# Silu of c in four pieces inside the projection, two opening blocks worked by input tile, longer warming runs: a transformer kernel on one core

## The reference, cut to what matters

```
h = rmsnorm(x, norm1_g)
proj = h @ w_in                     # dq, dk, dv, fq, fk, fv, fg
...                                 # two attentions, w_out, gated MLP
c_act = silu(c)                     # 1024 values
for l in 0, 1:
    sh_m, sc_m, g_m, sh_f, sc_f, g_f = split(c_act @ ada_w[l] + ada_b[l])
    h = modulate(rmsnorm(x, norm_g[l, 0]), sh_m, sc_m)
    y = conv mixer (l = 0) or latent attention (l = 1)
    x = x + g_m * rmsnorm(y, norm_g[l, 1])
    h = modulate(rmsnorm(x, norm_g[l, 2]), sh_f, sc_f)
    y = relu(h @ mlp_up_w[l]) ** 2 @ mlp_down_w[l]
    x = x + g_f * rmsnorm(y, norm_g[l, 3])
```

## Time and profile before

| | |
|---|---|
| median of 3 runs | 1792.23 us |
| profiled execution, its time | 1791.45 us |
| profiled execution, its span | 1789.7 us |
| time outside the span | 1.75 us |
| mean granted TensorE clock | 0.993 |
| weight blocks, KB each | 284, 512 |

### The profile page before, as it was taken

One profiled execution on the slowest core, in us unless ns is written; L12 is line 12 of the kernel. 1 busy time (PEld: TensorE's weight loads), 2 busy tenths in 40 slices (PEclk: granted clock), 3 DMA queues, 4 the chain that ended last, 5 costly groups with the idle time before them and its releaser, 6 DMA issues. The chain is left out here.

```text
span 1789.7 us, 22632 instructions
## 1 busy us (share of the span) xinstructions
PE 1746.8 (98%) x8124; PEld 1413.5 (79%) x8124; DVE 1094.8 (61%) x1603; ACT 632.2 (35%) x987; POOL 95.0 (5%) x155
## 2 busy tenths in 40 slices
PE   8989999999999999999999999999999999999996
PEld 7857677888888888887888888877767788888886
DVE  6676554655555576878656565667775865434354
ACT  4226444322222353244423142425444442323231
POOL 0000000000000000100100000010000100000001
PEclk9999999999999999999999999999999999999998
DMA  6421111444444434652245555521321234333221
GB/s 230 116 85 36 48 48 56 155 148 164 146 153 153 141 106 130 219 192 83 83 176 188 203 180 203 174 85 53 118 71 38 81 97 163 105 94 95 94 82 47
DMA packets 61951, 216.63 MB, mean 121 GB/s; under 512 B 7216, under 2 KB 9392, under 8 KB 61680
## 3 DMA queue, kind: packets, MB, share of 16 engines
q1 hardware_dynamic: 45072, 154.95, 25.7%
q0 software_dynamic: 16656, 60.04, 10.9%
q10 hardware_dynamic: 144, 0.59, 0.1%
HBM read 212.67 MB, written 2.10 MB: 120 GB/s over the span
## 5 line engine op out<-in xcount | busy, mean ns | idle before, releaser
L794 ACT ACTIVATE w_hi<-w_raw 128x1024 fp32r<-128x1024 f32 x284 | 299.0, 1054 | 409.0 <-PE psum L1952 372.1
L1950 PE MATMUL psum<-h_hi,w_hi 128*128 128x512 f32 x1080 | 421.4, 390 | 2.9 <-DVE h_lo L1200 2.9
L1952 PE MATMUL psum<-h_hi,w_lo 128*128 128x512 f32 x1080 | 420.2, 389 | 0.0
L1951 PE MATMUL psum<-h_lo,w_hi 128*128 128x512 f32 x1080 | 420.2, 389 | 0.0
L1175 DVE TENSOR_TENSOR w_lo<-w_raw,w_hi 128x1024 fp32r<-128x1024 f32 x284 | 347.2, 1223 | 116.6 <-ACT w_hi L794 108.7
L1950 PE MATMUL psum<-hid_hi,w_hi 128*128 128x512 f32 x736 | 286.3, 389 | 0.0
L1951 PE MATMUL psum<-hid_lo,w_hi 128*128 128x512 f32 x736 | 286.3, 389 | 0.0
L1952 PE MATMUL psum<-hid_hi,w_lo 128*128 128x512 f32 x736 | 286.3, 389 | 0.0
L1950 PEld LDWEIGHTS psum<-h_hi,w_hi 128*128 128x128 f32 x1080 | 202.7, 188 | 46.9 <-DVE h_lo L1200 3.8
L1951 PEld LDWEIGHTS psum<-h_lo,w_hi 128*128 128x128 f32 x1080 | 202.8, 188 | 42.3 <-issue 0.5
L1952 PEld LDWEIGHTS psum<-h_hi,w_lo 128*128 128x128 f32 x1080 | 202.7, 188 | 42.2
(11 more groups left out here) (342 smaller groups left out, 1964.5 us busy)
## 6 DMA issues: line engine op xcount, KB each, us to landing
w_raw<-in_wstream SPq DMA_DIRECT2D x284, 512.0 KB, 3.6
ada_raw<-in_ada POOLq DMA_DIRECT2D x112, 512.0 KB, 3.8
x<-in_xT SPq DMA_DIRECT2D x8, 256.0 KB, 5.1
outT<-x SPq DMA_DIRECT2D x16, 128.0 KB, 1.8
con<-in_consts SPq DMA_DIRECT2D x1, 1028.0 KB, 10.1
con<-in_rope ACTq DMA_DIRECT2D x1, 576.0 KB, 5.7
w_raw<-in_wstream SPq DMA_DIRECT2D x2, 256.0 KB, 3.7
c_row<-in_crow POOLq DMA_DIRECT2D x1, 512.0 KB, 4.0
```

The source lines that it names most:

```text
L794: act.activation(w_hi[:, slot, :], w_raw[:, slot, :], ACT.Copy).then_inc(whi_done, 1)
L1950: pe.matmul(bank, w_hi[:, slot, w], hi[:, ra + k, :], start=k == 0, stop=False)
L1951: pe.matmul(bank, w_hi[:, slot, w], lo[:, ra + k, :], start=False, stop=False)
L1952: mm = pe.matmul(bank, w_lo[:, slot, w], hi[:, ra + k, :], start=False, stop=k == nk - 1)
```

## The change

Three edits.

1. **Opening.** The first two weight blocks are worked together, input tile by input tile (kouter=2): for a tile PE runs four matmuls with h_hi, then two with h_lo. So both blocks are loaded and split in halves: first halves of blocks 0 and 1 after x tile 0, second halves after x tile 3; block 2 comes after x tile 7. DVE does the lo parts at tiles 1 and 3 of its loop: the second halves stand ahead of `lift` of tile 3. WARM_START goes from 15 to 18.
2. **Silu of c.** The exponential moves on ACT to block 0 of the five-block projection stage, with a wait for c_row. The three DVE steps run in four pieces of 128x256, one behind the `put` of each of blocks 1 to 4 of that stage. `values` loses `silu_c()`. The first use of c_row waits for the fourth piece.
3. **Warming.** NEW_WARM goes from 18 to 27.

The plan and the constants:

```diff
-WARM_START, WARM = 15, 9
+WARM_START, WARM = 18, 9
-NEW_WARM = 18
+NEW_WARM = 27
...
-    gemm("scaled", 3, "h", h, dst="proj", dst_at=0, qscale=True)
+    gemm("scaled", 3, "h", h, dst="proj", dst_at=0, qscale=True, kouter=2)
...
-    gemm("scaled", 5, "h", h, dst="proj", dst_at=3, qscale=True)
+    gemm("scaled", 5, "h", h, dst="proj", dst_at=3, qscale=True, silu=True)
```

SP, the opening:

```diff
-                if c < 2:
-                    half = slice(c * S, (c + 1) * S)
-                    sp.dma_start(w_raw[:, 0, half], wstream[0][:, half]).then_inc(raw_loaded[0] if c else raw_half, 16)
-                if c in OPEN_W:
-                    n = OPEN_W.index(c) + 1
-                    sp.dma_start(w_raw[:, n, :], wstream[n]).then_inc(raw_loaded[n], 16)
+                if c in (0, 3):
+                    half = slice(0, S) if c == 0 else slice(S, D)
+                    for n in range(2):
+                        sp.dma_start(w_raw[:, n, half], wstream[n][:, half]).then_inc(raw_loaded[n] if c else raw_half[n], 16)
+                if c == DT - 1:
+                    sp.dma_start(w_raw[:, 2, :], wstream[2]).then_inc(raw_loaded[2], 16)
```

ACT, in the projection stage behind `split_hi`, and what leaves `forget1`:

```diff
+                    if s.get("silu") and t.b == 0:
+                        act.wait_ge(ss_done, at_["ss"])
+                        act.wait_ge(c_loaded, 16)
+                        act.activation(c_exp, c_row[:, :], ACT.Exp, scale=-1.0).then_inc(c_step, 1)
...
-                    act.wait_ge(c_loaded, 16)
-                    act.activation(c_exp, c_row[:, :], ACT.Exp, scale=-1.0).then_inc(c_step, 1)
```

DVE, behind the `put` of a block, and the pieces themselves:

```diff
+                        if s.get("silu") and t.b >= 1:
+                            silu_c(t.b - 1)
...
+            def silu_c(i):
+                part = slice(i * D // 4, (i + 1) * D // 4)
+                dve.wait_ge(c_step, 2 * i + 1)
+                dve.tensor_scalar(c_exp[:, part], c_exp[:, part], 1.0, None, ALU.add).then_inc(c_step, 1)
+                dve.wait_ge(c_step, 2 * i + 2)
+                dve.reciprocal(c_exp[:, part], c_exp[:, part]).then_inc(c_step, 1)
+                dve.wait_ge(c_step, 2 * i + 3)
+                dve.tensor_tensor(c_row[:, part], c_row[:, part], c_exp[:, part], ALU.mult).then_inc(c_done, 1)
```

DVE, the opening and the values stages:

```diff
-                        if c < 2:
-                            half = slice(c * S, (c + 1) * S)
-                            dve.wait_ge(whi_done if c else whi_half, 1)
-                            dve.tensor_tensor(w_lo[:, 0, half], w_raw[:, 0, half], w_hi[:, 0, half].bitcast(F32),
-                                              ALU.subtract).then_inc(wlo_done if c else wlo_half, 1)
-                        lift(s, c)
-                        if c in OPEN_W:
-                            split_lo(OPEN_W.index(c) + 1, OPEN_W.index(c) + 1)
+                        if c == 1:
+                            lift(s, 0)
+                        if c in (1, 3):
+                            half = slice(0, S) if c == 1 else slice(S, D)
+                            for n in range(2):
+                                dve.wait_ge(whi_half if c == 1 else whi_done, n + 1)
+                                dve.tensor_tensor(w_lo[:, n, half], w_raw[:, n, half], w_hi[:, n, half].bitcast(F32),
+                                                  ALU.subtract).then_inc(wlo_half if c == 1 else wlo_done, 1)
+                        if c >= 1:
+                            lift(s, c)
+                        if c == DT - 1:
+                            split_lo(2, 2)
...
-                    if s["group"] == 1 and s["slot"] == 2:
-                        silu_c()
```

PE, in the part that works several blocks tile by tile:

```diff
+                opening = at_["n"] == 0
                 for t in blocks:
-                    pe.wait_ge(wlo_done, t.n + 1)
+                    if opening:
+                        pe.wait_ge(wlo_half, t.n + 1)
+                    else:
+                        pe.wait_ge(wlo_done, t.n + 1)
...
+                    if opening and k == nk // 2:
+                        pe.wait_ge(wlo_done, len(blocks))
```

More of the change, by code:

```diff
@@ L520, in build @@
         norm1_loaded = sem("norm1_loaded")
-        raw_half = sem("raw_half")
+        raw_half = [sem(f"raw_half{i}") for i in range(2)]
         whi_half = sem("whi_half")
@@ L884, in open_stage @@
                     act.activation(h_hi[:, c, :], x[:, c, :], ACT.Copy, scale=col(s["gain"], c)).then_inc(hi_done, 1)
-                    if c < 2:
-                        half = slice(c * S, (c + 1) * S)
-                        act.wait_ge(raw_loaded[0] if c else raw_half, 16)
-                        act.activation(w_hi[:, 0, half], w_raw[:, 0, half], ACT.Copy).then_inc(whi_done if c else whi_half, 1)
-                    if c in OPEN_W:
-                        split_hi(1, OPEN_W.index(c) + 1, None)
+                    if c in (0, 3):
+                        half = slice(0, S) if c == 0 else slice(S, D)
+                        for n in range(2):
+                            act.wait_ge(raw_loaded[n] if c else raw_half[n], 16)
+                            act.activation(w_hi[:, n, half], w_raw[:, n, half], ACT.Copy).then_inc(whi_done if c else whi_half, 1)
+                    if c == DT - 1:
+                        split_hi(1, 2, None)
                 for c in range(DT):
@@ L1179, in weighted @@
             def weighted(first, upto):
+                if first == 0:
+                    dve.wait_ge(c_done, 4)
                 for u in range(first, upto):
@@ L1185, in weighted @@
                                              accum_out=ada_sum[:, u:u + 1]).then_inc(ada_used, 1)
[L1187 to L1193, removed]
-                dve.tensor_tensor(c_row[:, :], c_row[:, :], c_exp, ALU.mult).then_inc(c_done, 1)
-                dve.wait_ge(c_done, 1)
+            def silu_c(i):
[6 more added lines that the diff above has]
+                dve.tensor_tensor(c_row[:, part], c_row[:, part], c_exp[:, part], ALU.mult).then_inc(c_done, 1)
             def lift(s, c):
@@ L1934, in step @@
                     slot = t.n0 % SPLIT
-                    halves = at_["n"] == 0 and isinstance(t.b, int) and t.b == 0
-                    if halves:
-                        pe.wait_ge(wlo_half, 1)
-                    else:
-                        pe.wait_ge(wlo_done, t.n + 1)
+                    pe.wait_ge(wlo_done, t.n + 1)
                     for q in range(s["nout"]):
@@ L1944, in step @@
                         for k in range(nk):
-                            if halves and k == nk // 2:
-                                pe.wait_ge(wlo_done, 1)
                             if t.j == 0 and q == 0:
```

1 line of the change is left out of this document (removed).

## The result

Four executions of the changed kernel gave 1779.12 to 1781.64 us, median 1779.67; four of the kernel before, beside them, had a median of 1791.90. The ratio is 0.9934 with a 95% interval of 0.9916 to 0.9951: faster, by 12.2 us. The profiled execution took 1779.12 us, its span is 1777.2 us, 12.5 less than before.

The account below looks back on a forecast made before the run. PE, busy 98% of the span, was taken as the bound. Gains of 2.6 + 6.6 + 1.8 + 1.85 = 12.85 us took the profiled 1791.45 to 1778.6, and 0.78 for the median gave 1779.4 us; range 1777.6 to 1783.0.

Parts of the forecast that it names:

- case (a): Whole kernel: the forecast itself, with all its gains, ending at 1779.4 us; chance 0.60.
- opening: First three weight blocks: PE starts at 7.7 us, runs without stalls and ends at 24.0 instead of 26.64; gain 2.6 us.
- wait on vrow: End of the values stages: without the silu on DVE, scores start at 111.0 instead of 117.61; gain 6.6 us.
- clock at the scores: First scores and filler matmuls: after a wait of only 0.9 us PE keeps the full clock; gain 1.8 us.
- two norms: Two renewed norms: nine more warming products each keep the clock full; gain 0.95 and 0.9, together 1.85 us.
- rival (c): Opening gains only half, through a late half of block 1 or tile 3's lo part: 1780.5 us; chance 0.12.
- The cover: Projection: DVE's wait of 3.19 us for PE per block hides a silu piece of 2.6 us, so it costs nothing.
- rival (e): Projection: each piece's reciprocal takes the whole 6.55 us, DVE runs late and the scores start later: 1798 us; chance 0.02.
- Rival (f): Scores: something other than vrow holds them, so 6.6 and 1.8 us are not gained: 1787.8 us; chance 0.02.
- rival (d): First score units: ACT and DVE work swallows the regained clock, 1.8 us back: 1781.2 us; chance 0.06.
- Rival (b): Both norms: the clock falls all the same, as 0.55 to 1.4 us stay idle; 1.85 back, 1781.2 us; chance 0.13.
- Rival (b2): First norm: its clock fall has another cause than 2.64 us of idle and stays; 0.95 back, 1780.3 us; chance 0.05.

Follow-up runs that it names:

- the second set: The changed kernel run again without any change, against the kernel before: median 1780.14 us, ratio 0.9934.
- the 18-product run: Changed kernel with 18 instead of 27 warming products at the norms: 1782.26 us, ratio 0.9949 to the kernel before.
- pieces in the old place: Changed kernel with the four silu pieces one behind the other in the values stage of group 1, slot 2: 1789.16 us, ratio 0.9984 to the kernel before.

## Why the prediction was right, and where its terms were off

The forecast was 1779.4 us; measured were 1779.67, and 1780.14 in the second set. The gain was forecast as 12.8 us and came out at 12.2; that the time lies nearer to the forecast than the gain does is luck, since the kernel before, run beside it, was itself 0.3 us faster than the median that the forecast started from. It was case (a), and by its steps, each read from the trace of the kernel after:

| term | forecast us | measured us |
|---|---|---|
| opening | 2.6 | 2.14 |
| wait on vrow | 6.6 | 6.58 |
| clock at the scores | 1.8 | 1.67 |
| two norms | 1.85 | 1.75 |
| sum | 12.85 | 12.14 |
| the span | | 12.5 |

**Opening.** It came out between case (a), 2.6, and rival (c), 1.5. The start was forecast for 7.7 and came at 8.28, and the late half of block 1 explains that: it landed at 6.71, not at the 6.14 taken from x tile 1. The steps behind it cost what was forecast: ACT's pass ends at 7.34, DVE's goes from 7.37 to 8.06, and PE starts 0.22 us later. In the three profiles with this opening in which PE stood waiting, for 0.56 to 1.00 us, it started just as long behind DVE's last lo part (8.27 and 8.48, 8.53 and 8.75, 8.59 and 8.81).

The six more short matmuls also took longer than forecast: 36 took 6.87 us where 30 took 5.34, 1.5 us more for 0.7. Their own price was right: from start to start they take 0.112 us at the end of the warming, as at the norms. But the first ones take 0.213, and this lasted until 7.0 us in the kernel after and until 5.2 in the kernel before:

```profile
3.00:6.00 3.00, 3.00 (x16) 3.00 (x16) 1.31 (x3) 1.24 (x2) 0.00 (x0) 1.00 0.99 283
7.10:8.10 1.00, 1.00 (x11) 1.00 (x11) 0.69 (x1) 0.78 (x2) 0.00 (x0) 1.00 1.00 385
```

These windows of the kernel after have 16 short matmuls in 3 us and 11 in 1 us, those cut by an edge counted too. Over the fourteen profiles the pace doubles between 4.5 and 7.3 us, so 30 took 5.02 to 6.24 us and 36 took 6.10 to 7.00. "Costs nothing" held all the same in the kernel after: the last of them starts at 8.16, just ahead of the real work. Of the eight profiles with this opening and 18 products, in which real work starts at 8.14 to 8.81, the warming held PE clearly in one, that of the opening alone: DVE's lo part ended at 7.71 there, and PE started at 8.14, 0.2 us later than the hand-over asks for.

The rest of the step held: the three blocks took 24.50 - 8.28 = 16.2 us (forecast 16.3), and tile 3's lo part was there in time, with 1 us of room instead of 0.4: DVE does it right at 11.56, and PE wants it at 8.28 + 4.08 + 0.91 = 13.3.

**Silu.** The wait went as forecast, 6.58 for 6.6, and 0.84 us are left for 0.9. A piece took 2.46 us for 2.6, its reciprocal of 256 columns 1.75, just as the line between 2 and 1024 columns gave. The cover held: DVE waited for PE 1.0 to 1.2 us ahead of the puts behind the first three pieces. The run with the whole silu shows that even rival (e)'s reciprocal of 6.55 us, once, costs nothing there; four of them were not tried. Rival (f) is refuted by the silu part alone, which took the wait away.

**Clock at the scores.** 1.67 for 1.8, and not swallowed: rival (d) is refuted by the kernel before with warming products in the wait, where the same 1.67 us appeared with nothing else changed, and stayed to the fifth unit. The first norm's real work, 1.92 us earlier there (845.27 for 847.19), still has it.

**Norms.** 0.90 + 0.85 for 0.95 + 0.9; idle left is 0.63 and 1.49 for 0.55 and 1.4. Rival (b) is refuted: seven profiles with 27 products hold fourteen norms, all between 17.13 and 17.19 us, none with a fall of the clock. The other side is less simple than the prediction had it. Five profiles have 18 products, that of the kernel before among them. Their second norm, behind 3.50 us of idle, fell in all five, for about 3.4 or 6.8 us, and took 18.00 to 19.11 us. Their first, behind 2.64 us, fell in three and kept its clock in two (17.18 and 17.20 us). So the nine products are worth about 3/5 x 0.9 = 0.5 us at the first norm and 18.64 (the mean of the five) - 17.15 = 1.5 us at the second, 2.0 together, near what the 18-product run lost (2.1 to 2.6) and above what 27 products alone brought (1.42, known to 1.6 either way). The 1.85 was near it for a wrong reason: it took one execution's fall at the first norm for certain and one execution's short fall at the second for the rule.

The Trainium skill (TensorE: Matmul & The Clock Gate, Why this matters for your kernels) warns only of idle gaps somewhat longer than the first norm's. The runs don't agree with it as a safe bound: 2.64 us at the first norm was followed by a fall in three of five profiles, and 2.61 us with 22 products in the one there is. Gaps of 0.63, 1.49 and 1.74 us were followed by none. Rival (b2), that the fall at the first norm has another cause than the idle and stays, is refuted by the fourteen norms.

**The parts together.** Alone they brought 7.34 + 1.52 + 1.42 = 10.3 us, together 11.5 (second set) to 12.2. The missing 1.2 to 1.9 us were not traced to one place, and they lie within the noise: the intervals of the three parts are 1.6 to 2.4 us to either side. The execution profiled of the silu part had the long slow stretch at the second norm, which alone is 1.1 us. In the trace 12.5 - 12.14 = 0.4 us belong to no term; 0.3 of them lie between the fifth unit of the scores (10.4 us earlier than before) and the first norm (10.7 earlier), and what they are was not followed up.

**What stays open.** Whether 15 warming products at the start are better than 18: one profile and overlapping times can't say it. How the clock can fall in some executions and not in others of the same stretch. And whether it is the idle time alone that counts at the norms: more warming products shorten it and lengthen the work ahead of it, and no run changed one without the other.

## What to carry to other kernels

An operation whose result is needed only much later (here the silu of c) is worth moving to a stage where its engine waits anyway; whether it is cut in pieces matters only if a whole one holds up the engine that sets the pace, and a put that came 5 us late did not do that here. Where PE stands still ahead of heavy work, fill the gap with warming products until the idle left is no longer than those behind which no fall was seen (here 0.6 to 1.7 us): too few leave the clock to chance, and some too many cost less than their length where tiles pace the work behind them. And don't take one execution for the rule, neither for the clock nor for the landing of a transfer: in the opening both moved by more from execution to execution than three warming products cost, so a start read once says little on what a change there is worth.

## What the runs showed of the hardware

**The clock falls with PE fully busy, in some executions.** Stage `forget2` runs eight matmuls with eight output rows and then twenty that stream eight columns. In four of the thirteen profiles beside that of before (27 products alone, pieces in the old place, 36, 22) the clock fell behind them, in the others not. That these narrow matmuls are the cause is not shown, since no run was made without them. The pieces in the old place, PE and windows:

```profile
92.59 2.32 PE L2328 MATMUL psum<-con,log_f 128*8 128x512 f32 x8
94.84 2.40 PE L2333 MATMUL psum<-log_f,con 128*128 128x8 f32 x20
```

```profile
97.00:98.00 1.00, 1.00 (x6) 0.85 (x6) 0.49 (x2) 0.00 (x0) 0.00 (x0) 0.78 0.00 0
98.00:99.00 1.00, 1.00 (x4) 0.71 (x4) 1.00 (x2) 0.00 (x0) 0.00 (x0) 0.50 0.00 0
```

PE is busy at 1.00 throughout and the granted clock is 0.50 from about 97.6 to 101. With 36 and 22 products the scores start at 111.04 and 110.98 instead of 108.88, and about 0.5 of these 2.1 us are their later start in the opening, so such a fall costs some 1.6 us. Part of the spread between executions of one kernel (1789.75 to 1794.29 us over 21 of the kernel before) may come from this; their traces were not taken.

**The first warming products run at half pace, for a time that varies.** At the start of the kernel a short matmul takes 0.213 us from start to start; then the pace goes to 0.112, that of the norms. The change came at 4.5 to 7.3 us in the fourteen profiles, while PE ran nothing but warming products, and it is where the trace's first record of the granted clock begins, at full. The view of windows has 1.00 before it too, so in the opening it is the pace that tells the clock, not that column.

**The time at which the third 256 KB transfer lands varies**: ACT's pass on the half of block 1 began at 6.36 to 7.24 us in eight profiles, and by 5.4 in one, with the same transfers issued ahead of it.
